# A two-block transformer kernel in split fp32: FFN products of 512 columns, and a second mixer with its side work in another order

## The reference, cut to what matters

```python
h = h + 0.5 * swiglu(rms_norm(h), ffn1_w13, ffn1_w2)      # 1024 -> 2 x 2816 -> 1024
u = rms_norm(h)
z, xbc, dt, cq, ckv, kr, gates = split(u @ w_in)
y_ssd = ssd_branch(z, xbc, dt, ...) @ w_ssd_out           # scan; y * silu(z); 2048 -> 1024
y_mla = mla_branch(cq, ckv, kr, ...) @ w_mla_out          # 8 heads, causal softmax, 1024 -> 1024
h = h + (g1 * y_ssd + g2 * y_mla) @ w_o
h = h + 0.5 * swiglu(rms_norm(h), ffn2_w13, ffn2_w2)
```

## Time and profile before

| what | value |
|---|---|
| median of 3 runs | 3530.79 us (3530.78 to 3533.06) |
| the profiled execution, its own time | 3533.26 us |
| its span, first to last instruction | 3531.4 us |
| mean granted TensorE clock | 0.976 of full speed |
| PE busy | 3215.9 us, 91% of the span |
| DVE busy | 2353.5 us, 67% |
| ACT busy | 1614.2 us, 46% |
| second block, from its first product | 1926.4 us to the end |

### The profile page before, as it was taken

One profiled execution on the slowest core, in us unless ns is written; L12 is line 12 of the kernel. 1 busy time (PEld: TensorE's weight loads), 2 busy tenths in 40 slices (PEclk: granted clock), 3 DMA queues, 4 the chain that ended last, 5 costly groups with the idle time before them and its releaser, 6 DMA issues. The chain is left out here.

```text
span 3531.4 us, 52045 instructions
## 1 busy us (share of the span) xinstructions
PE 3215.9 (91%) x19034; PEld 2543.7 (72%) x19034; DVE 2353.5 (67%) x4532; ACT 1614.2 (46%) x3554; POOL 1136.9 (32%) x1243
## 2 busy tenths in 40 slices
PE   6998989988789898898977999999999999999999
PEld 5895444443378854444424999899899999899899
DVE  6776666766577566676774657767666657767665
ACT  3643333333355433333333445656444445656443
POOL 1315677777612076677773000002000000002000
PEclk7998999999999999999999999999999999999999
DMA  7689999999965699999997554344455554344454
GB/s 296 209 278 368 409 409 409 409 409 409 393 229 196 222 409 409 409 409 409 409 409 289 175 179 144 126 143 141 142 185 184 182 180 141 127 143 140 141 185 162
DMA packets 258299, 937.22 MB, mean 265 GB/s; under 512 B 29312, under 2 KB 30720, under 8 KB 257792
## 3 DMA queue, kind: packets, MB, share of 16 engines
q0 software_dynamic: 161280, 587.27, 42.3%
q1 hardware_dynamic: 96768, 346.62, 28.9%
HBM read 932.73 MB, written 1.05 MB: 264 GB/s over the span
## 5 line engine op out<-in xcount | busy, mean ns | idle before, releaser
L769 PE MATMUL M<-rows,diag 128*128 128x512 f32 x2048 | 971.6, 610 | 190.5 <-DMA rows<-in_expert_v_dram,expert 175.3
L334 DVE TENSOR_TENSOR w_low<-ring,w_high 128x1024 fp32r<-128x1024 f32 x560 | 689.5, 1234 | 414.8 <-ACT w_high L326 411.9
L769 PEld LDWEIGHTS M<-rows,diag 128*128 128x128 f32 x2048 | 365.5, 190 | 744.9 <-DMA rows<-in_expert_v_dram,expert 411.2
L1291 DVE CUSTOM_DVE_ANT_0 rows<-rows,G 128x1024 f32<-128x1024 f32 x512 | 616.6, 1219 | 425.1 <-DMA rows<-in_expert_u_dram,expert 340.6
L353 PE MATMUL G<-x_high,w_high 128*128 128x256 f32 x2576 | 761.2, 295 | 45.2 <-DVE w_low L334 15.1
L326 ACT ACTIVATE w_high<-ring 128x1024 fp32r<-128x1024 f32 x560 | 588.8, 1055 | 336.3 <-PE G L353 311.1
L356 PE MATMUL G<-x_high,w_low 128*128 128x256 f32 x2576 | 739.0, 287 | 0.0
L355 PE MATMUL G<-x_low,w_high 128*128 128x256 f32 x2448 | 703.9, 288 | 0.0
L489 POOL DMA_INDIRECT rows<-in_expert_u_dram,expert x512 | 482.3, 942 | 339.3 <-DVE expert L1274 139.1
L353 PEld LDWEIGHTS G<-x_high,w_high 128*128 128x128 f32 x2576 | 504.6, 196 | 57.0 <-issue 35.3
L489 POOL DMA_INDIRECT rows<-in_expert_v_dram,expert x512 | 482.3, 942 | 185.9 <-issue 121.9
(11 more groups left out here) (378 smaller groups left out, 4904.9 us busy)
## 6 DMA issues: line engine op xcount, KB each, us to landing
ring<-in_stream_dram SPq DMA_DIRECT2D x632, 512.0 KB, 3.3
ada_ring<-in_ada_stream_dram POOLq DMA_DIRECT2D x80, 512.0 KB, 4.8
rows<-in_ada_stream_dram POOLq DMA_DIRECT2D x16, 512.0 KB, 16.1
rows<-in_expert_u_dram,expert POOLq DMA_INDIRECT x512, 15.9
rows<-in_expert_v_dram,expert POOLq DMA_INDIRECT x512, 16.0
ada_ring<-in_stream_dram SPq DMA_DIRECT2D x8, 512.0 KB, 6.2
spare<-in_stream_dram SPq DMA_DIRECT2D x6, 512.0 KB, 7.8
sq<-in_stream_dram SPq DMA_DIRECT2D x4, 512.0 KB, 9.7
```

Of the source, the lines that this page charges most:

```text
L334: dve.tensor_tensor(T["w_low"][:, part, :], T["ring"][:, place.slot(chunk, slots), :], T["w_high"][:, part, :].bitcast(F32), ALU.subtract) ...
L769: mm = pe.matmul(M[:, 2 * t + half, :], T["diag"][:, n % 4, :], T["v_rows"][:, n % SLOTS, half * 512:(half + 1) * 512], start=(h == 0 and ...
L1291: dve.tensor_tensor_reduce(row, row, TOKENS, 1.0, 0.0, ALU.mult, ALU.add, T["hid"][:, r, k:k + 1]).then_inc(sem["u_used"], 1)
```

## The change

In the FFNs the high and low halves of an activation lie in one tile (`x_halves`, `ff_halves`, `attn_halves`), so that one matmul with `w_high` reads both as 512 columns and writes a whole bank: its first half is high x high, its second is low x high. The `w_low` matmul of 256 columns adds into the first half. For each tile there are so two matmuls and two weight loads in place of three and three, over the same 768 columns. The two halves of the bank are added afterwards: in the first 44 groups ACT copies the second half to SBUF (L1982) and DVE adds the first to it (L2239, L2250) before its old step; in the 8 output groups DVE scales both halves and adds them (L2263, L2264).

In the second mixer the table puts `z_gate` first in its step; `cb` alternates between two banks (PT and SC) in place of one; softmax of head 0 moves to the last v step and that of head j + 1 to ssd_out j, with turn_probs j in the same step and values j in the next one; `attn_low` comes one step earlier and the last `merged_low` ahead of the cut of the next chunk; and the first two outputs are made in turns (`halved_pair`): tiles 0 to 5 of output 0, then of output 1, then tiles 6 and 7 of each. Within the pair PE signals `w_used` once only, at tile 6 of output 1.

```diff
+def halved_pair(pe, w, T, sem, halving, outs, high, low, kt, ready, full, place=UNSHIFTED):
+    base, split = w.at, kt - 2
+    w.take(2 * kt)
+    for ks in (range(split), range(split, kt)):
+        for turn, out in enumerate(outs):
+            for k in ks:
+                before = base + turn * kt + k
+                chunk, r = divmod(before, TILES)
+                n = halving.number[chunk]
+                part = place.part(n)
+                if r == 0 or k == ks[0]:
+                    pe.wait_ge(sem["low_ready"], n + 1)
+                tile = slice(r * P, (r + 1) * P)
+                if turn == 0:
+                    ready(k)
+                mm = pe.matmul(out, T["w_high"][:, part, tile], high(k), start=(k == 0), stop=False)
+                if turn == 1 and k == split:
+                    w.free(mm, before)
+                pe.matmul(out, T["w_high"][:, part, tile], low(k), start=False, stop=False)
+                mm = pe.matmul(out, T["w_low"][:, part, tile], high(k), start=False, stop=(k == kt - 1))
+            if ks[-1] == kt - 1:
+                mm.then_inc(full, 1)
...
+def wide_products(pe, w, T, sem, halving, out, pair, kt, ready, place=UNSHIFTED):
+    for k in range(kt):
+        before = w.at
+        w.take(1)
+        chunk, r = divmod(before, TILES)
+        n = halving.number[chunk]
+        part = place.part(n)
+        if r == 0 or k == 0:
+            pe.wait_ge(sem["low_ready"], n + 1)
+        tile = slice(r * P, (r + 1) * P)
+        if ready:
+            ready(k)
+        if k < kt - 1:
+            mm = pe.matmul(out, T["w_high"][:, part, tile], pair(k), start=(k == 0), stop=False)
+            w.free(mm, before)
+            pe.matmul(out[:, 0:S], T["w_low"][:, part, tile], pair(k)[:, 0, :], start=False, stop=False)
+        else:
+            mm = pe.matmul(out[:, 0:S], T["w_low"][:, part, tile], pair(k)[:, 0, :], start=False, stop=False)
+            w.free(mm, before)
+            mm = pe.matmul(out, T["w_high"][:, part, tile], pair(k), start=False, stop=True)
+    return mm
...
 _side(STEP_OF["dt", 0] + 2, "acum", 0)
+for _j in range(KX):
+    _side(STEP_OF["z", _j] + 1, "z_gate", _j)
...
-for _j in range(KX):
-    _side(STEP_OF["z", _j] + 1, "z_gate", _j)
...
-    _side(STEP_OF["ssd_out", _j], "gate_tanh", _j)
-    _side(STEP_OF["ssd_out", _j], "softmax", _j)
-    _side(STEP_OF["ssd_out", _j] + 1, "turn_probs", _j)
-    _side(STEP_OF["ssd_out", _j] + 2, "values", _j)
-SIDE[STEP_OF["mla_out", 1]].remove(("values", 7))
-SIDE[STEP_OF["mla_out", 0]].remove(("turn_probs", 7))
-SIDE[STEP_OF["mla_out", 0]].remove(("values", 6))
-SIDE[STEP_OF["ssd_out", 7]] += [("values", 6), ("turn_probs", 7), ("values", 7)]
-for _j in range(MLA_HEADS):
     _side(STEP_OF["v", _j], "ssd_halves", 2 * _j)
     _side(STEP_OF["v", _j], "ssd_halves", 2 * _j + 1)
-    _side(min(STEP_OF["ssd_out", _j] + 3, STEP_OF["ssd_out", 7]), "attn_low", _j)
+_side(STEP_OF["v", 7], "softmax", 0)
+for _j in range(MLA_HEADS):
+    _at = STEP_OF["ssd_out", _j]
+    _side(_at, "gate_tanh", _j)
+    if _j < MLA_HEADS - 1:
+        _side(_at, "softmax", _j + 1)
+    _side(_at, "turn_probs", _j)
+    if _j >= 1:
+        _side(_at, "values", _j - 1)
+_side(STEP_OF["ssd_out", 7], "values", 7)
+for _j in range(MLA_HEADS):
+    _side(min(STEP_OF["ssd_out", _j] + 2, STEP_OF["ssd_out", 7]), "attn_low", _j)
     _side(STEP_OF["mla_out", _j], "merged_high", _j)
-    _side(STEP_OF["mla_out", _j] + 1, "merged_low", _j)
-SIDE[STEP_OF["out", 0]].remove(("merged_low", 7))
+    _side(min(STEP_OF["mla_out", _j] + 1, STEP_OF["mla_out", 7]), "merged_low", _j)
...
+        def project_wide(g, pair, kt, ready=None):
+            bank_free_2(pe, g)
+            wide_products(pe, w, T, sem, HALVING_2, G[:, g % GB, 0:2 * S], pair, kt, ready, place
+                          ).then_inc(g_full, 1)
...
-        def ffn(g0, g_out, i, high, low, beside, beside_out):
+        def ffn(g0, g_out, i, pair, beside, beside_out):
 
             at = 0 if i == 0 else KF
             for j in range(2 * KF):
-                project_halved(g0 + j, high, low, KD,
-                               x_halves(i) if j == 0 and not (opening and i == 0) else None)
+                project_wide(g0 + j, pair, KD, x_halves(i) if j == 0 and not (opening and i == 0) else None)
                 beside(j)
             for j in range(KD):
 
-                project_halved(g_out + j, lambda k: ff_high[:, k, :], lambda k: ff_low[:, k, :], KF,
-                               (lambda k: pe.wait_ge(sem["ff_low_ready"], at + k + 1)) if j == 0 else None)
+                project_wide(g_out + j, lambda k: T["ff_halves"][:, :, k, :], KF,
+                             (lambda k: pe.wait_ge(sem["ff_low_ready"], at + k + 1)) if j == 0 else None)
                 beside_out(j)
...
-            if g >= 1:
-                pe.wait_ge(sem["cb_ready"], g)
+            if g >= 2:
+                pe.wait_ge(sem["cb_ready"], g - 1)
             b, c = T["bc"][:, g, :], T["bc"][:, SSD_GROUPS + g, :]
-            pe.matmul(PT[:, 0:S], b[:, 0:P], c, start=True, stop=True)
-            pe.matmul(PT[:, S:S + P], b[:, P:S], c[:, P:S], start=True, stop=True
+            bank = (PT, SC)[g % 2]
+            pe.matmul(bank[:, 0:S], b[:, 0:P], c, start=True, stop=True)
+            pe.matmul(bank[:, S:S + P], b[:, P:S], c[:, P:S], start=True, stop=True
...
-            pe.wait_ge(sem["qk_ready"], h + 1)
             if h == 0:
+                pe.wait_ge(sem["qk_ready"], MLA_HEADS)
...
+            elif (kind, j) == ("out", 0):
+                for turn in (g, g + 1):
+                    bank_free_2(pe, turn)
+                halved_pair(pe, w, T, sem, HALVING_2, [G[:, turn % GB, 0:S] for turn in (g, g + 1)], x_high,
+                            x_low, KD, lambda k: pe.wait_ge(sem["merged_low_ready"], k + 1), g_full, place)
+            elif (kind, j) == ("out", 1):
+                pass
             elif kind == "out":
-                project_halved(g, x_high, x_low, KD, (lambda k: pe.wait_ge(
-                    sem["merged_low_ready"], k + 1)) if j == 0 else None)
+                project_halved(g, x_high, x_low, KD)
...
+            def second_half(g, out):
+                act.wait_ge(g_full, g + 1)
+                act.activation(out, G[:, g % GB, S:2 * S], ACT.Copy).then_inc(sem["silu_ready"], 1)
             for j in range(KF):
                 act_halves.ahead(act, g0 + 2 * j)
-                evacuated(act, g_free, g0 + 2 * j)
-                act.activation(silu[:, j % 2, :], silu[:, j % 2, :], ACT.Silu).then_inc(sem["silu_ready"], 1)
+                second_half(g0 + 2 * j, silu[:, j % 2, :])
                 act_halves.ahead(act, g0 + 2 * j + 1)
                 if j >= 1:
                     high(j - 1)
+                evacuated(act, g_free, g0 + 2 * j)
+                act.activation(silu[:, j % 2, :], silu[:, j % 2, :], ACT.Silu).then_inc(sem["silu_ready"], 1)
+                if j >= 2:
+                    act.wait_ge(sem["ff_low_ready"], i * KF + j - 1)
+                second_half(g0 + 2 * j + 1, ff[:, j % 2, :])
...
-                dve.tensor_tensor(silu[:, j % 2, :], G[:, g % GB, 0:S], rstd[:, :], ALU.mult
+                dve.wait_ge(sem["silu_ready"], 3 * (i * KF + j) + 1)
+                link(dve.tensor_tensor(silu[:, j % 2, :], G[:, g % GB, 0:S], silu[:, j % 2, :], ALU.add))
+                dve.tensor_tensor(silu[:, j % 2, :], silu[:, j % 2, :], rstd[:, :], ALU.mult
                                   ).then_inc(g_free[g % GB], 1)
                 evacuated(dve, g_free, g)
                 dve_halves.ahead(dve, g + 1)
                                                   in1=T["rstd_ssd"][:, :], op0=ALU.mult, op1=ALU.mult))
                 if j >= 1:
                     low(j - 1)
-                if j >= 2:
-                    dve.wait_ge(sem["ff_low_ready"], i * KF + j - 1)
-                dve.wait_ge(sem["silu_ready"], i * KF + j + 1)
-                dve.wait_ge(g_full, g + 2)
-                dve.tensor_tensor(ff[:, j % 2, :], G[:, (g + 1) % GB, 0:S], silu[:, j % 2, :], ALU.mult
+                dve.wait_ge(sem["silu_ready"], 3 * (i * KF + j) + 3)
+                link(dve.tensor_tensor(ff[:, j % 2, :], G[:, (g + 1) % GB, 0:S], ff[:, j % 2, :], ALU.add))
+                dve.tensor_tensor(ff[:, j % 2, :], ff[:, j % 2, :], silu[:, j % 2, :], ALU.mult
...
-                link(dve.tensor_tensor(silu[:, j % 2, :], G[:, g % GB, 0:S], rstd[:, :], ALU.mult))
-                dve.scalar_tensor_tensor(out=x[:, j, :], in0=silu[:, j % 2, :], scalar=0.5,
+                if j >= 1:
+                    evacuated(dve, g_free, g - 1)
+                for n, half in enumerate(both(g)):
+                    link(dve.tensor_tensor(silu[:, n, :], half, rstd[:, :], ALU.mult))
+                link(dve.tensor_tensor(silu[:, 0, :], silu[:, 0, :], silu[:, 1, :], ALU.add))
+                dve.scalar_tensor_tensor(out=x[:, j, :], in0=silu[:, 0, :], scalar=0.5,
...
-                if j == 0:
```

(20 more changed lines are left out.)

9 lines of the change are left out of this document (4 added, 5 removed).

## The result

The changed kernel takes 3499.93 us (3499.07 to 3500.73, 4 runs) where the kernel before takes 3531.84 us (3530.78 to 3533.06, 4 runs) on the same chip: ratio 0.9909, 95% interval 0.9896 to 0.9922, **31.9 us faster**. The forecast was 48.6 us: right in direction and inside the range of 8 in 10 (3457 to 3502), but at its upper end and outside the forecast's own 3474 to 3490.

A forecast was written before the change was run, and what follows sets the result against it. PE's matmul rate was taken to bound the FFNs, other engines the mixer's stalls. FFNs 29.6 - 5.8 = 23.8 us plus mixers 24.8 made 48.6 us, giving 3482 us (own range 3474 to 3490; 8 in 10: 3457 to 3502).

The forecast's parts named there:

- rival (d): FFNs: become a loop of DVE and ACT and the kernel gets slower, around 3560 us in a mild form; chance 0.04.
- (a): FFN products: weight load hides behind the long matmul, a 512 takes 216 ns, 21 us more gain, 3461; chance 0.20.
- (c): FFN products: the extra goes with the columns, a 512 takes 240 ns, products gain 0, 3512 us; chance 0.06.
- Rival (b): Mixer: stalls are only handed on, half of the 24.8 us gain is lost, 3494 us; chance 0.17.
- The z gate: Mixer: with the gate ahead, both PE stalls (4.10 us) and the half-speed clock (1.7) go, 5.8 us per layer.
- FFN products: FFN tiles: one 512 and one 256 matmul take 346 ns instead of 360, saving 29.6 us over 2112 tiles.
- The edges: FFN starts and ends: longer chains behind the last output group cost 3.8 us, fifth chunks 2.0; 5.8 in all.
- Heads and pair: Second mixer: moved softmaxes give 4.3 us per layer, outputs 0 and 1 made in turns 2.3.
- the new wait: Output 2: late w_used makes PE wait 2.1 us, which could bring back the low clock, even odds and 1.7 us.
- both old waits: Output 0 of the kernel before: PE waits of 2.12 and 1.70 us, after which the clock fell.

The follow-up runs named there:

- the appended series: Changed kernel with series of split matmuls appended behind its last product: 512 columns take 227.5 ns among their like, 512 and 256 in turns 353 ns a pair.
- late_z: Changed kernel with the z gate back at its old place, behind the other side work of its step: 3514.09 us, 13.0 slower than the changed kernel beside it.
- grouped: Changed kernel with each chunk's FFN products in two groups, first those of 512 columns, then those of 256: 3495.49 us, ratio 0.9891 to the kernel before.
- no_pair: Changed kernel with outputs 0 and 1 of the second mixer's last projection computed one after the other again: 3499.54 us, 1.6 under the changed kernel beside it.

## Why the prediction was right and wrong

**Right in its mechanism.** PE's rate stayed the bound of the FFNs, with DVE at 82% against the forecast's 85; rival (d) did not come. Rivals (a) and (c) fall by the appended series: 512 columns cost 227 ns among their like, neither 216 nor 240. The Trainium skill's rule (TensorE: Matmul & The Clock Gate, Back-to-back issue gap) gives 216 for a 512 on its own; no series here shows that, and the measured 227 decides. In the kernel's turns a 512 takes 235, which is near to (c)'s price without (c)'s reason. Rival (b), mixer stalls handed on, did not come either: the mixers gave more than was forecast. The z gate (forecast 11.6 us for both layers, stage 11.8, undone in `late_z` 12.3 in that stage) is shown by undoing it.

**Inside the range by luck.** The range reached up to 3502 to take in rival (b), half of the mixer's gain lost. The time landed there although (b) was wrong, because half of the products' gain was missing, a shortfall of a size that no rival named.

**The step that failed is a size**: in "FFN products", the "14 ns less per tile, 29.6 us for 2112". Two numbers in it were off. Its 120 ns for a 256 came from one early stretch; the old 704 tiles that read the attention's halves took 118.7 a matmul, 356.1 a tile. The old tiles together took 2.3 us less than the forecast had, of the 14.5 that are missing. And its 227 for a 512 is the price of a 512 among its like, while the kernel puts a 256 behind each. Old and new tile by what they read: x 360.8 to 352.5, attention's halves 356.1 to 351.5, ff 359.9 to 351.2 ns (means over the steps at full clock, those over 300 ns, one per output at most, left out). With 704 tiles of each that is 5.8 + 3.2 + 6.1 = **15.1 us**, not 29.6. `grouped` shows that 2 to 3 ns of an x or ff tile hang on the order, 3.8 us in all. The rest of the shortfall is open: in groups of eight a tile still takes 349 ns or more, in the kernel and in the appended series, where its two matmuls alone make 347 (the forecast's 346 is 1 ns under that sum). What makes the attention's halves different was not tested.

**The edges** were put at 5.8 us; the stages leave 15.1 - 7.7 = 7.4. Those that can be read one by one come to 5.5: behind FFN 1 the wait grew from 0.56 to 1.48, the forecast's 0.92 exactly, in both layers; layer 1 waits 0.69 for x, forecast 1.0; the fifth chunk waits 1.09 longer in layer 0 (4.35 in place of 3.26) and 0.77 in layer 1, where the forecast had 0.5 at each of four FFNs and the two FFNs 2 show none; and from PE's last product to the end it is 4.61 in place of 3.52 us. Not forecast: the first of these fifth chunks brings 3.4 us at clock 0.50, and on the other side the opening was at 0.50 for only 2.9 us of its products (to 1930.9) where it had been for 5.5 us (to 1931.9). The other 1.9 us of the 7.4 the runs do not place.

**Heads and pair** together were put at 6.6 us a layer and gave 7.5 and 8.0. But the split was wrong: the pair brought 0.6 where the clock held and about nothing on average, not 2.3; that the new wait might bring the low clock back it had foreseen, at even odds, where 5 of 16 waits did. The forecast charged it with both old waits of 2.12 and 1.70 us. `no_pair` shows that the second is gone without it: without the pair the stage still is 6.95 us shorter than before in layer 0. The heads explain 4.2 of that by the rows (waits of 2.73 and 0.64 down to 0.84, and the low clock's 1.7), as forecast. The other 2.7 are not separated by any run; the last merged half's new place, one step up, is the edit that touches the wait.

Summed against the traces: -15.1 products, +7.4 edges, -27.3 mixers, +1.6 first block is -33.4, the spans' 3531.4 to 3498.0.

## What to carry to other kernels

A rate read from a series of equal matmuls is not the rate of two kinds in turns: take it from the order that the kernel will run, or measure that order by itself. Group products of one width where the data allow it, and let the first group wait only for the operand it reads. And when several edits meet at one wait, undo each alone before crediting it: here the pair of outputs was credited with two waits, and one of them was gone without it. A wait behind which the clock may fall is worth counting over several executions, for one trace shows only one outcome.
